# Turning the memory rows: products with a scaled diagonal, or rows scaled in place and transposed

## The reference, cut to what matters

```python
def rmsnorm(x, g):
    x32 = x.astype(jnp.float32)
    var = jnp.mean(x32 * x32, axis=-1, keepdims=True)
    return (x32 * lax.rsqrt(var + NORM_EPS) * g.astype(jnp.float32)).astype(x.dtype)

def memory_attention(q, mem_n, w_mem_kv):
    kv = mem_n @ w_mem_kv
    mk, mv = jnp.split(kv, 2, axis=-1)
    ...

def first_block(...):
    ...
        h = rmsnorm(x, norm_pre[l])
        proj = h @ w_in[l]
        ...
        mem_n = rmsnorm(mem, norm_mem[l])
        y_x = memory_attention(q_x.reshape(bsz, seq, XATTN_HEADS, XATTN_HEAD_DIM), mem_n, w_mem_kv[l])
```

## Time and profile before

| what | value |
|---|---|
| median of 3 runs | 2856.13 us |
| the three runs | 2853.51, 9218.42, 2856.13 us |
| the profiled execution, its own time | 2855.17 us |
| its span, first to last instruction | 2853.4 us |
| mean granted TensorE clock | 0.996 of full speed |
| TensorE / VectorE / ScalarE / GpSimd busy | 99% / 49% / 37% / 12% |

### The profile page before, as it was taken

How to read it: one execution, slowest core, us unless ns; L and a number is a source line. 1 busy time by engine, 2 the same in 40 slices (tenths; PEclk the granted TensorE clock), 3 DMA queues, 4 the chain that set the end, 5 groups by cost and what they waited for, 6 DMA issues and landing times.

```text
span 2853.4 us, 38419 instructions
## 1 busy us (share of the span) xinstructions
PE 2817.0 (99%) x15552; PEld 2351.8 (82%) x15552; DVE 1397.1 (49%) x2525; ACT 1063.1 (37%) x1848; POOL 328.3 (12%) x581
## 2 busy tenths in 40 slices
PE   7999999999999999999999999999999999999998
PEld 7888777888889888888888889887777777777888
DVE  5686634436236545455544335325544453445534
ACT  6233233455225333322222335434444443233322
POOL 6356044100000000001000000000000000000000
PEclk9999999999999999999999999999999999999999
DMA  7566455323434555466664424542322223222423
GB/s 198 124 192 121 116 119 123 107 76 97 173 96 156 165 153 156 137 182 199 179 190 122 168 97 131 128 96 67 78 67 71 67 67 91 80 81 82 148 96 118
DMA packets 448207, 350.49 MB, mean 123 GB/s; under 512 B 73420, under 2 KB 404012, under 8 KB 443808
## 3 DMA queue, kind: packets, MB, share of 16 engines
q1 hardware_dynamic: 412816, 241.93, 30.3%
q0 software_dynamic: 35216, 106.11, 12.8%
HBM read 322.88 MB, written 22.81 MB: 121 GB/s over the span
## 4 chain that ended last, share of the span: by engine, by line
PE 95%; DVE 3%; DMA 1%; ACT 1%; issue 0%; POOL 0%; SPq 0%; DVEq 0%; ACTq 0%
PE bank L3504 56%; PE bank L3544 16%; PE bank L3514 4%; PE bank L3567 2%; PE bank L3462 2%; PE bank L2308 1%; PE bank L2359 1%; PE bank L2335 1%; PE bank L2380 1%; DMA ring<-in_w_in 1%; PE bank L630 1%; PE bank L625 1%; PE bank L2428 1%; PE bank L694 1%; PE bank L3437 1%; PE bank L2354 0%
## 5 line engine op out<-in xcount | busy, mean ns | idle before, releaser
L3656 DVE TENSOR_TENSOR ring_parts<-ring,ring_hi 128x1024 fp32r<-128x1024 f32 x416 | 503.9, 1224 | 705.0 <-ACT ring_hi L3615 700.0
L3615 ACT ACTIVATE ring_hi<-ring 128x1024 fp32r<-128x1024 f32 (+1 forms) x420 | 437.4, 1052 | 582.8 <-DMA ring<-in_w_in 299.8
L3504 PE MATMUL bank<-A_parts,ring_hi 128*128 128x512 f32 x1552 | 622.5, 401 | 0.4 <-DVE ring_parts L3656 0.3
L3504 PE MATMUL bank<-A_parts,ring_parts 128*128 128x512 f32 x1552 | 607.4, 391 | 0.0
L3504 PE MATMUL bank<-X_parts,ring_hi 128*128 128x512 f32 x1360 | 531.6, 391 | 0.0
L3504 PE MATMUL bank<-B_parts,ring_hi 128*128 128x512 f32 x1224 | 478.8, 391 | 0.0
L3504 PEld LDWEIGHTS bank<-A_parts,ring_hi 128*128 128x128 f32 x1552 | 292.8, 189 | 67.1 <-issue 9.2
L3504 PEld LDWEIGHTS bank<-A_parts,ring_parts 128*128 128x128 f32 x1552 | 292.6, 189 | 63.1
L3504 PEld LDWEIGHTS bank<-X_parts,ring_hi 128*128 128x128 f32 x1360 | 256.8, 189 | 51.8 <-issue 0.5
L3504 PE MATMUL bank<-B_parts,ring_parts 128*128 128x512 f32 x752 | 292.7, 389 | 0.0
L3504 PEld LDWEIGHTS bank<-B_parts,ring_hi 128*128 128x128 f32 x1224 | 230.0, 188 | 52.4 <-issue 5.9
(11 more groups left out here) (561 smaller groups left out, 3877.2 us busy)
## 6 DMA issues: line engine op xcount, KB each, us to landing
ring<-in_w_in SPq DMA_DIRECT2D x288, 512.0 KB, 3.8
ring<-in_w_out SPq DMA_DIRECT2D x96, 512.0 KB, 3.6
work<-in_w_ada POOLq DMA_DIRECT2D x96, 512.0 KB, 4.8
ring<-in_w_in SPq DMA_DIRECT2D x48, 256.0 KB, 3.7
ring<-in_w_mem_kv SPq DMA_DIRECT2D x16, 512.0 KB, 4.1
x_keep<-X POOLq DMA_DIRECT2D x8, 1024.0 KB, 4.9
X<-x_keep POOLq DMA_DIRECT2D x8, 1024.0 KB, 10.2
X<-in_x SPq DMA_DIRECT2D x4, 1024.0 KB, 10.3
```

The costliest lines, as they stand in the source:

```text
L3504: mm = nc.tensor.matmul(K.ps(st)[0:w + (t["beside"] or 0), 0:t["n"]], lhsT=wp[:, j, :], rhs=columns(ap, kk), start=first, stop=end)
L3615: nc.scalar.activation(slot_view[key](ring_hi), slot_view[key](ring), ACT.Copy).then_inc(s_hi, 1)
L3656: nc.vector.tensor_tensor(lo, slot_view[key](ring), slot_view[key](ring_hi), ALU.subtract).then_inc(s_lo, 1)
```

## The change: what it does

VectorE no longer makes a diagonal for the memory rows. It multiplies the rows themselves, in place, by the reciprocal of their root mean square, in four pieces of 128x512 for each 128 rows, and raises `mem_rows_scaled` after each. TensorE turns them with `nc.tensor.transpose` against the plain identity, and waits ahead of each bank for the piece that it reads. The x rows keep the diagonal. VectorE's `m_rstd` no longer waits for `x_turn`, which it did because the diagonals share their buffer.

```diff
     def pe_m_turn(pe, st):
         tt = st[1]
-        pe.wait_ge(s_diag, TT + tt + 1)
-        turn_rows(pe, st, mem_rows[:, tt, :], diag[:, tt, :])
+        for k4 in range(KT // 4):
+            pe.wait_ge(s_mem_scaled, tt * (KT // 4) + k4 + 1)
+            bk.take(pe, st, k4)
+            for j in range(4):
+                kk = 4 * k4 + j
+                mm = nc.tensor.transpose(ps(st, k4)[:, j * P:(j + 1) * P], mem_rows[:, tt, kk * P:(kk + 1) * P], K.ident[:, :])
+            mm.then_inc(bk.full_sem(st, k4), 1)
...
@@ vec_scale
-        nc.vector.tensor_scalar(diag[:, no % TT, :], K.ident[:, :], r1, None, ALU.mult).then_inc(s_diag, 1)
+        if no < TT:
+            nc.vector.tensor_scalar(diag[:, no, :], K.ident[:, :], r1, None, ALU.mult).then_inc(s_diag, 1)
...
     def vec_m_rstd(vec, L, st):
         tt = st[1]
-        vec.wait_ge(*bk.filled(("x_turn", tt), KT // 4 - 1))
-        vec_scale(vec, L, mem_rstd[:, tt:tt + 1], TT + tt)
+        r1 = mem_rstd[:, tt:tt + 1]
+        vec_scale(vec, L, r1, TT + tt)
+        for c in range(D // NC):
+            cols = slice(c * NC, (c + 1) * NC)
+            nc.vector.tensor_scalar(mem_rows[:, tt, cols], mem_rows[:, tt, cols], r1, None, ALU.mult).then_inc(s_mem_scaled, 1)
```

More of the change, by code:

```diff
@@ L377, in block1 @@
     s_pre, s_par, s_tab = K.sem("norm_pre_loaded"), K.sem("b1_params"), K.sem("b1_tables")
-    s_mem = K.sem("mem_loaded")
+    s_mem, s_mem_scaled = K.sem("mem_loaded"), K.sem("mem_rows_scaled")
     K.s_mem = s_mem
```

## The result

Sixteen timed runs of the changed kernel have a median of **2850.97 us** (2849.09 to 2855.64), sixteen of the kernel before 2857.12. The ratio is 0.9978 with a 95% interval of 0.9972 to 0.9985: 6.3 us faster, between 4.3 and 8.0. The profiled execution spans 2848.4 us against 2853.4. The forecast was 2852.7, from a gain of 3.4.

What follows compares the result with a forecast made beforehand. TensorE was taken to bound the kernel; two turns at 1.79 instead of 3.49 us save 3.4 us, with VectorE's added 3.2 us hidden. From the median 2856.13 that gives 2852.7 us, range 2848 to 2858 for 8 in 10.

Steps and rivals of the forecast that it cites:

- The bound: TensorE, busy 2817.0 of 2853.4 us, sets the end; a microsecond less there is worth one if operands are not late.
- The size of a turn: TensorE's turn of 128 memory rows falls from 3.49 to 1.79 us, twice, saving 3.4 us.
- rival (a): Scalings of 0.69 us make VectorE's weight split late; TensorE waits 1.1 us, gain 2.3, time 2853.8; chance 5%.
- a sign: The forecast is wrong if VectorE's scalings take more than 0.56 us, the limit for no TensorE wait on the split.
- the delay of 1.3 us: VectorE's evictions of turn 0 start at 69.96 instead of 68.64, moving the next splits from 76.73 to 78.1.
- rival (b): GpSimd's DMA issues block VectorE's scalings; TensorE waits 6.6 us, 3.2 slower, 2859.3; chance 2%.
- rival (c): TensorE's clock falls to 1.2 GHz for the tile after a turn, up to 11 us more, 2864; chance 2%.
- rival (d): A later TensorE wait, candidate the 1.5 us ahead of 184.20, takes back the gain; if all, 2856.1; chance 8%.
- rival (e): Transposes do not halve TensorE's instruction count in the turns and cost the same 3.49 us; 2856.1; chance 1%.
- the sum: Only the two turns' 3.4 us come off: 2851.8 us from the profiled execution, 2852.7 from the median 2856.13.
- The range: For 8 in 10, 2848 to 2858 us, including some 1.5 us for loads and instruction fetches that fall differently.
- the forecast's own interval: 2849.5 to 2855.5 us for the forecast case, resting on a 2.6 us spread of single runs before; chance 82%.

Runs made afterwards that it cites:

- e5: Kernel before with the products of both memory-row turns done twice; 1.0024 of before, 6.9 us slower, 7.9 at equal clock.
- e11: The change plus X's row group 3 turned by transposes of GpSimd-scaled rows, and ScalarE's join square ahead of its load wait; 2848.94 us, 0.9975 of before.
- e2: Kernel before with transposes of unscaled memory rows, diagonals still made, division by root mean square left out; 0.9976 of before.
- e4: Kernel before, unedited, timed against itself; ratio 1.0000.
- e7: Kernel before with ScalarE's square of X's third row group moved ahead of its first weight-load wait at the join; 0.9997 of before.
- e8: Kernel before with sixteen idle one-column products at the start of TensorE's program; 0.9993 of before.
- e0: The change again, no edit, timed beside the kernel before; 0.9983, 4.9 us faster.
- e1: The change with its transposes made ordinary products with the plain identity again, rows still scaled in place; 1.0003 of before.
- e6: The change plus X's row group 3 turned by transposes of rows that GpSimd scaled in place; 0.9970 of before.
- e3: The change with turn 0 by products with the plain identity and only turn 1 by transposes, both of scaled rows; 0.9985 of before.
- e9: The change with sixteen idle one-column products at the start of TensorE's program; 0.9990 of before, 2.9 us faster.
- e10: The change a third time, no edit, on the chip of the padded versions; 0.9985 of before, 4.3 us faster.

## Why the prediction was right, point by point

**The bound: right.** A microsecond off TensorE was a microsecond off the time, in both directions: the turns gave 3.66 us at 180 us, e5 took 7.1 at 143 us and 6.9 (4.6 to 9.4) at the end.

**The size of a turn: a little off.** The forecast had 1.79 us, from sixteen pitches of 0.109 and a hand-over; measured are 1.66 and 1.67. The 32 records have 270 to 273 ns. The last transpose overlaps with the next product, and the hand-over that I added isn't there. The 3.49 us of before, under 32 pitches of 0.111, held the same overlap, so the two sides of the difference were not counted alike. Saved: 3.65 us, not 3.4.

**VectorE and the late split, rival (a): right to hide it.** Each scaling took 0.43 to 0.47 us of VectorE in this profile where I took 0.48, and up to 0.54 in others (2.15 us for four in e11); single records reach 0.598 us, over the 0.56 that I named as a sign, but they overlap, and no wait followed. The splits start at 67.06 (I had 67.60) and leave a slack of 0.8 us (I had 0.6). The evictions start at 69.33 and take 0.62 each, so the next splits (76.40) are even ahead of their place before, 76.73; the delay of 1.3 us that I carried along in full is gone by then.

**GpSimd, rival (b): did not happen.** All eight scalings started within its burst of issues and took at most 0.598 us. But the two do cost each other something, as all profiles together show. Without scalings (before, e2, e4, e5, e7, e8) the sixteen issues take 8.39 to 8.44 us. With them, either the burst is longer (8.90 to 9.22 in after, e0, e1 and e6, where four scalings take 1.68 to 1.95), or it is not (8.42 to 8.43 in e3, e9, e10 and e11) and the first four scalings take 2.05 to 2.15. That is 0.5 to 0.8 us for GpSimd or some 0.3 for VectorE, both hidden here.

**The clock, rival (c): did not happen.** 1.00 from 69 to 81 us. The sentence of the Trainium skill cited in the prediction, that the fast clock does not engage for transposes ("TensorE: Matmul & The Clock Gate", "Part 4: PE-mode transpose"), doesn't hold in this run either.

**Given back later, rival (d): did not happen**, and the opposite did. The wait for `u_blocks` kept its 1.5 us and came 3.84 us earlier.

**Half the count, rival (e):** 32 records for 64, as forecast.

**The step that was mis-sized** is the sum: 3.4 for 6.3 us (4.3 to 8.0). It had the turns as its only term. It lacks the join of blocks 1 and 2. The prediction had "some 1.5 us for loads and instruction fetches that fall differently", but only as width, with either sign. Here it is a term of its own: a TensorE program with fewer instructions moved one program packet away from a load that is waited for, 3.41 less 2.08 = 1.3 us of waiting, and up to 0.9 us behind it, where before's records ran in part at half the clock and those of the change did so in e10 alone of three profiles. With 3.65 that makes 5.0 to 5.9, beside 5.4 at equal clock with an uncertainty of 0.7; in e9 the term is taken out again and 3.0 are left. What remains up to 6.3 is within the interval of the ratio. The range, and the forecast's own interval from 2849.5 to 2855.5, both held the time, in part by luck: the kernel before came out 1.0 us above the median that the forecast started from, which took up a part of what the sum lacked, and the spread of 2.6 us that the interval rests on came from two runs, where fifteen lie between 2853.51 and 2863.37.

**Open:** what made e3's load a little late (ScalarE waits 0.65 us, TensorE 2.47) without a program packet near it. Why the load lands 1.0 to 1.4 us later when the packet begins 0.3 to 0.8 us behind its issue, but not when it begins 0.8 us ahead; I didn't try to move it in small steps. Why the records at the join ran at half the clock in e10. Why e8 gains only 0.7 us at equal clock with a join that is 2.2 shorter. For e5 the sum closes in its profile: 7.1 of turns, 2.4 at and behind the wait for `u_blocks`, less the join's 2.2, is 7.3 us, beside 7.9 at equal clock.

## What to carry to other kernels

On an engine that sets the end, count instructions and not bytes or columns: an f32 product with a diagonal is two instructions for each call, an f32 transpose one, and a scaling that a less busy engine can do in place ahead of time makes the exchange possible. Before you trust a difference of a few microseconds between two profiles, compare the kernels at equal granted clock, and add a version that is only padded to the old instruction count: it separates what the edit does from what its program's new position does. Where an engine waits for a load ahead of work that doesn't need it (here the square behind `a00`), the order can be turned round so that a late load is hidden: it made the join 2.6 us shorter in e7's profile, though the times of e7 and e11 don't show a gain from it.

## What the runs showed of the hardware

- A program packet of 16 KB that began 0.3 to 0.8 us after the issue of a 64-KB load, with a 1-MB store under way beside it, went with a landing 1.0 to 1.4 us later (median of the two loads in the stretch 5.3 to 5.7 us in five profiles, against 4.3 in eight; e3 had 5.3 without such a packet). The store landed later as well (5.9 to 6.3 us against 4.5). Sixteen idle products at the start of TensorE's program brought it about or took it away.
- Four scalings of 128x512 f32 in place: VectorE 1.68 to 2.15 us, GpSimd 8.29 us. Eight of them inside a burst of sixteen GpSimd DMA issues made either the burst 0.5 to 0.8 us longer or four of the scalings some 0.3 us.
- Sixteen f32 transposes between tile products cost TensorE 1.66 us, less than their busy time of 1.91.
